# A two-layer MoE network with a gated recurrent mixer: the recurrent mixer's last projections, GpSimd's order and the start of the output projections are rearranged

## What is computed

```python
def short_conv_mixer(xn, w_in, conv_w, w_out):            # layer 0
    bgate, cgate, h = jnp.split(xn @ w_in, 3, axis=-1)
    u = depthwise_conv(cgate * h, conv_w, (1, 1))
    return (bgate * u) @ w_out

def rglru_direction(uh, w_r, b_r, w_i, b_i, lam, reverse):
    r = sigmoid(einsum(uh, w_r) + b_r)                    # blocks of 256 channels
    i = sigmoid(einsum(uh, w_i) + b_i)
    log_a = -RG_C * r * softplus(-lam)
    a = exp(log_a)
    gated = sqrt(-expm1(2 * log_a)) * (i * u)
    return associative_scan(_linear_combine, (a, gated), reverse=reverse)

def rglru_mixer(xn, ...):                                 # layer 1
    y_branch, u = jnp.split(xn @ w_in, 2, axis=-1)
    y_branch = gelu(y_branch)
    u = depthwise_conv(u, conv_w, (2, 1)) + conv_bias
    h = rglru_direction(uh, ..., False) + rglru_direction(uh, ..., True)
    return (y_branch * h) @ w_out

for i in range(DEPTH):
    h = h + mix
    h = h + hier_moe(rmsnorm(h, norm_ffn[i]), ...)        # 32 experts, three 2 MB matrices each
    h = h + sigmoid(rmsnorm(h, norm_ple[i]) @ w_ple_gate[i] + b) * (p[i] @ w_ple[i])
```

## Time and profile before

| | us |
|---|---|
| median of 3 runs | 2106.71 |
| lowest and highest | 2106.17, 2112.98 |
| the profiled execution, its own time | 2108.99 |
| its span | 2107.2 |
| TensorE busy | 1968.6 (93%) |
| layer 0's mixer ends, output projection begins | 190.9 |
| layer 1's mixer, first full projection block to last | 848 to 1018 |
| layer 1's output projection begins | 1021.2 |
| layer 1's experts begin | 1105.8 |

### The profile page before, as it was taken

One profiled execution on the slowest core, in us unless ns is written; L12 is line 12 of the kernel. 1 busy time (PEld: TensorE's weight loads), 2 busy tenths in 40 slices (PEclk: granted clock), 3 DMA queues, 4 the chain that ended last, 5 costly groups with the idle time before them and its releaser, 6 DMA issues.

```text
span 2107.2 us, 21306 instructions
## 1 busy us (share of the span) xinstructions
PE 1968.6 (93%) x8286; PEld 970.6 (46%) x8286; DVE 760.3 (36%) x2018; ACT 419.0 (20%) x871; POOL 100.8 (5%) x128
## 2 busy tenths in 40 slices
PE   7999999999999799988999999999979899998997
PEld 3444555444444235433464444444424564644554
DVE  3111353221111143454345421111115448656674
ACT  2000010111110124166111111111013432113342
POOL 0000000000000010013300000000010000000000
PEclk9999989999999999999999999999989999996999
DMA  6187179999999981210537999999995212210000
GB/s 276 40 166 280 60 301 402 429 427 429 428 428 428 421 340 40 74 46 0 248 141 326 405 428 429 427 428 428 428 398 232 85 71 80 80 40 1 17 15 11
DMA packets 46323, 512.79 MB, mean 243 GB/s; under 512 B 5248, under 2 KB 5248, under 8 KB 17152
## 3 DMA queue, kind: packets, MB, share of 16 engines
q1 hardware_dynamic: 37760, 481.38, 56.1%
q0 software_dynamic: 8448, 29.89, 3.6%
HBM read 484.90 MB, written 26.35 MB: 243 GB/s over the span
## 4 chain that ended last, share of the span: by engine, by line
PE 80%; DVE 7%; DMA 6%; issue 4%; ACT 2%; POOL 1%; SPq 0%; DVEq 0%; POOLq 0%
PE ps L925 20%; PE ps L964 9%; PE ps L468 8%; PE ps L898 7%; PE ps L562 5%; PE ps L1316 5%; PE ps L1750 5%; DMA ring<-in_wexp 4%; PE ps L1479 3%; PE ps L2068 3%; PE ps L1510 2%; PE ps L1949 2%; PE ps L989 1%; PE ps L2112 1%; PE ps L2086 1%
## 5 line engine op out<-in xcount | busy, mean ns | idle before, releaser
L925 PE MATMUL ps<-ring,arena 128*48 128x512 f32 x1568 | 404.5, 604 | 43.1 <-issue 28.6
L925 PEld LDWEIGHTS ps<-ring,arena 128*48 128x48 f32 x1568 | 121.7, 125 | 243.9 <-issue 242.4
L938 DVE TENSOR_TENSOR arena<-arena,ps 48x512 f32<-48x512 f32 x64 | 44.1, 690 | 465.9 <-ACT arena L932 465.8
L964 PE MATMUL ps<-ring,arena 128*48 128x512 f32 x800 | 181.7, 592 | 2.4 <-issue 2.4
L898 PEld LDWEIGHTS ps<-arena,h 128*128 128x128 f32 x1024 | 158.6, 190 | 44.6 <-issue 44.6
L898 PE MATMUL ps<-arena,h 128*128 128x192 f32 (+1 forms) x1024 | 174.3, 325 | 0.0
L468 PE MATMUL ps<-arena,ring 128*128 128x512 f32 x384 | 165.0, 592 | 1.0 <-DVE arena L305 1.0
L925 PE MATMUL ps<-arena 128*48 128x512 f32 x480 | 159.4, 612 | 1.0 <-issue 1.0
L1750 PE MATMUL ps<-ring,arena 128*128 128x512 f32 (+3 forms) x384 | 135.2, 507 | 0.0
L932 ACT ACTIVATE arena<-ps 48x512 f32<-48x512 f32 x64 | 37.9, 592 | 479.6 <-PE ps L925 467.6
L562 PE MATMUL ps<-ring,arena 128*128 128x512 f32 x256 | 115.7, 608 | 7.0 <-DVE arena L500 3.9
(11 more groups left out here) (278 smaller groups left out, 2112.3 us busy)
## 6 DMA issues: line engine op xcount, KB each, us to landing
ring<-in_wexp SPq DMA_DIRECT2D x148, 2048.0 KB, 19.6
arena<-in_wexp SPq DMA_DIRECT2D x44, 2048.0 KB, 22.6
ring<-in_wall SPq DMA_DIRECT2D x28, 2048.0 KB, 8.6
y_d<-arena POOLq DMA_DIRECT2D x60, 192.0 KB, 7.1
yo_d<-arena SPq DMA_DIRECT2D x2, 4032.0 KB, 42.0
xs_d<-h POOLq DMA_DIRECT2D x8, 512.0 KB, 3.9
ring<-in_wall SPq DMA_DIRECT2D x2, 1536.0 KB, 6.8
h<-in_x SPq DMA_DIRECT2D x4, 512.0 KB, 9.5
```

What stands on the lines that cost most here:

```text
L925: mm = pe.matmul(outs[m], xeT[:, e_ // 4 % 2, k, e_ % 4 * CAP:(e_ % 4 + 1) * CAP], ws[m][:, k, :], start=(k == 0), stop=(k == KT - 1))
L938: dve.tensor_tensor(hh[0:CAP, e_ % 2, :], sl[0:CAP, e_ % 2, :], banks[1][64:64 + CAP, :], ALU.mult).then_inc(S["hh"], 1)
L964: mm = pe.matmul(outs[c], hT_of(e_ % 2)[:, k, :], w[:, k, c * 512:(c + 1) * 512], start=(k == 0), stop=(k == 3))
```

## The change

Three edits, in source order.

1. `pe_out` (both layers) no longer waits for all eight channel blocks ahead of the first product. Instead each of the eight matmuls of `product(0, 0)` waits for the block that it reads, with a floor: layer 0 waits for count 7 before the first seven and for 8 before the last; layer 1 waits for 5 before the first five, then for 6, 7 and 8. The floor is what frees PSUM bank 0.
2. `pe_mixer_b`: the first channel block of the y quarter (block 8 for d = 0, block 12 for d = 1) is computed in the middle of the gates, after c = 3. The other three blocks stay behind the gates.
3. `pool_mixer_b`: the first four products L1614 move in front of the last four sums, and the last four products alternate with them: sum 4, product 4, sum 5, product 5, and so on.

No instruction but waits is added or taken away.

```diff
--- before.py
+++ after.py
@@ -559,10 +559,11 @@
                 if i >= 1:
                     pe.wait_ge(S["op_add"], 8 * k + 2 * i + c - 1)
                 for kk in range(KT):
+                    if i == 0 and c == 0:
+                        pe.wait_ge(*((S["b_y"], max(kk + 1, 5)) if k else (S["a_gT"], max(kk + 1, 7))))
                     mm = pe.matmul(banks[c][:], gT[:, kk, i * P:(i + 1) * P], w[:, kk, :], start=(kk == 0), stop=(kk == KT - 1))
                 mm.then_inc(S["op_mm"], 1)
 
-            pe.wait_ge(S["b_y"] if k else S["a_gT"], 8)
             product(0, 0)
             product(0, 1)
             turn_half(pe, n, 0, 0)
@@ -1466,10 +1467,10 @@
             for key in (("b", 0), ("b", 1), ("gates", 0), ("b", 2), ("gates", 1), ("b", 3)):
                 sp_load(sp, key)
 
-        def pe_project(pe, q, at=0):
+        def pe_project(pe, q, at=0, to=4):
             w = w8(("b", q))
             pe_unit(pe, ("b", q))
-            for c4 in range(at, 4):
+            for c4 in range(at, to):
                 p_ = 4 * q + c4
                 if 4 <= p_ < 12:
                     pe.wait_ge(S["bu"], p_ - 3)
@@ -1509,7 +1510,9 @@
                         for k in range(2):
                             mm = pe.matmul(banks[4 + g % 4][:], w[:, a, blk, k, m * P:(m + 1) * P], uc[:, 2 * blk + k, :], start=(k == 0), stop=(k == 1))
                         mm.then_inc(S["b_gm"], 1)
-                pe_project(pe, 2 + d)
+                    if c == 3:
+                        pe_project(pe, 2 + d, 0, 1)
+                pe_project(pe, 2 + d, 1)
 
         def act_mixer_b(act):
             for c in range(8):
@@ -1596,22 +1599,34 @@
                         o.then_inc(S["b_sc"], 1)
 
         def pool_mixer_b(pool):
-            for d in range(2):
-                for hf in range(2):
-                    for cc in range(4):
-                        c = 4 * hf + cc
-                        k = 8 * d + c
-                        pool.wait_ge(S["b_gs"], 2 * k + 2)
-                        pool.tensor_tensor(bI[hf][:, cc, :], bI[hf][:, cc, :], uc[:, c, :], ALU.mult).then_inc(S["b_iu"], 1)
-                    if d == 1:
-                        for cc in range(4):
-                            c = 4 * hf + cc
-                            pool.wait_ge(S["b_sc"], 8 + c + 1)
-                            pool.tensor_tensor(hs[:, c, :], hs[:, c, :], bT[:, cc, :], ALU.add).then_inc(S["b_hs"], 1)
-            for c in range(8):
+            def gated(d, hf):
+                for cc in range(4):
+                    c = 4 * hf + cc
+                    k = 8 * d + c
+                    pool.wait_ge(S["b_gs"], 2 * k + 2)
+                    pool.tensor_tensor(bI[hf][:, cc, :], bI[hf][:, cc, :], uc[:, c, :], ALU.mult).then_inc(S["b_iu"], 1)
+
+            def both(c):
+
+                pool.wait_ge(S["b_sc"], 8 + c + 1)
+                pool.tensor_tensor(hs[:, c, :], hs[:, c, :], bT[:, c % 4, :], ALU.add).then_inc(S["b_hs"], 1)
+
+            def product(c):
                 pool.wait_ge(S["by"], c + 1)
                 pool.wait_ge(S["b_hs"], c + 1)
                 pool.tensor_tensor(yT[:, c, :], yT[:, c, :], hs[:, c, :], ALU.mult).then_inc(S["b_y"], 1)
+
+            gated(0, 0)
+            gated(0, 1)
+            gated(1, 0)
+            for c in range(4):
+                both(c)
+            gated(1, 1)
+            for c in range(4):
+                product(c)
+            for c in range(4, 8):
+                both(c)
+                product(c)
 
 
         QK = ar(4096, 17, 512)
```

## The result

| | before | after |
|---|---|---|
| median, us | 2107.9 (4 runs) | 2091.94 (4 runs) |
| lowest and highest | 2106.17, 2112.98 | 2084.6, 2094.43 |
| ratio of the times, 95% interval | | 0.9917 [0.9899, 0.9936] |
| the profiled execution, its own time | 2108.99 | 2084.6 |

A second session gave the changed kernel 2095.19 us (6 runs) against 2109.15, ratio 0.9935 [0.9914, 0.9955]. By the medians it is 16.0 and 14.0 us faster; 15.1 was forecast. The two intervals together reach from 9.5 to 21.3 us. The profiled execution is the fastest of its four and must not be read as the result: its span is 24.4 us shorter.

The account below looks back on a forecast made before the run. TensorE, busy 1968.6 of 2107.2 us, was taken as the bound, leaving only gaps and low clock to win. 5.7 (layer 0) + 9.4 (layer 1) = 15.1 us off the 2106.71 median gave 2091.6 us; range 2084 to 2098 (8 in 10).

Parts of the forecast that it names:

- What decides: Layer 1's output projection: product(0, 1) waits for the load of ("out", 1, 1), used at 1016.9 instead of 1029.16, 12.3 us earlier.
- The gates: Layer 1's gates: blocks 8 and 12 fill both 6.20 us gaps, saving 9.0 and 9.4 us.
- The close fit: Direction 0's gates: block 8 and four groups cover TensorE until ScalarE's first sigmoid, 0.65 us to spare.
- The last product: End of layer 1's mixer: GpSimd's last product brings b_y to 8 at 1008.8, 12.3 us earlier than 1021.1.
- The turns: Last half of layer 1's mixer: each GpSimd op ahead of a waiting VectorE op delays it 0.95 us, 10.0 in all.
- cheaper-pairs rival: Last half's L1582 and L1584 don't take turns with GpSimd; last product at 1003.6, time 2086.5 us; chance 0.15.
- Issue to use: Layer 1's second output-weight load: 8.04 us from the DMA's issue to its use by product(0, 1).
- Low clock behind the new gap: Layer 1's product(0, 1): after 7.1 us idle it runs partly at 1.2 GHz, costing 2.9 us, range 1.5 to 4.
- layer 1 term: Layer 1's output projection: 12.3 us from the earlier load less 2.9 of low clock, net 9.4 us.
- Layer 0: Layer 0's output projection: the 3.9 us gap and 1.8 us of slow clock go, 5.7 us.
- absorbing rival: Expert stages: a DMA start that doesn't move swallows one or both gains, 2101.0 to 2106.7 us; chance 0.09.
- The clock stays low: Rival, layer 1's output products: 1.2 GHz persists for the seven remaining products, 48.1 us more, 2136.8 us; chance 0.05.

Follow-up runs that it names:

- e2_layer1: Only the finer waits of edit 1, in layer 1 alone, against the kernel before: 2108.42 us, ratio 0.999.
- e5_slot: Changed kernel with the second half of layer 1's output weights in ring slot 3 instead of slot 2: 2085.48 us, ratio 0.9886.
- e3_blocks: Only edit 2, the projection block between the halves of the gates, against the kernel before: 2096.58 us, ratio 0.9936.
- e7_oldpool: Changed kernel with GpSimd's old order, so edits 1 and 2 without 3: 2092.58 us, ratio 0.9912.
- e6_slot_oldpool: Changed kernel with the output weights' second half in ring slot 3 and GpSimd's old order: 2091.82 us, ratio 0.9915.
- e4_gpsimd: Only edit 3, GpSimd's new order, against the kernel before: 2106.62 us, ratio 0.9981.
- e8_dve: Against e5_slot, the eight products with the y branch run on VectorE, four behind each half's scans: 2083.57 us, ratio 0.987.
- e1_layer0: Only the finer waits of edit 1, in layer 0 alone, against the kernel before: 2103.93 us, ratio 0.9967.
- e9_dve_noslot: As e8_dve, but the output weights' second half stays in the slot that counts as used until the last product: 2086.41 us, ratio 0.9881.

## Why the prediction was right, point by point

- **What decides.** The step on which the forecast stood, that the load of ("out", 1, 1) ends the wait, holds: the bracket is in the profile (6.51 us forecast as about 7), e2_layer1 shows the early start worth nothing alone, and e5_slot wins 6.7 us of stage by giving this load another slot.
- **The gates.** 9.0 and 9.4 us, right to some tenths: from the first gate matmul to the first output product are 990.33 - 880.47 = 109.9 us, and 999.6 - 889.5 = 110.1 was forecast. The close fit held, no bracket opened.
- **The last product.** 1008.8 forecast in the times of the kernel before; measured 1000.0, which is 1009.1 with the 9.06 us by which the first gate matmul moved. The turns were forecast to cost 10.0 us ahead of the last scan's end, and the lengthened ops there add up to 10.2. The price of 0.95 us was right for the pairs too, which no row had shown: five long ops of 1.64 to 1.76 in the pairs. With it the cheaper-pairs rival falls. The rule of the Trainium skill (SBUF — State Buffer, Who interferes with whom), that an op with two SBUF inputs excludes a GpSimd op that reads SBUF, agrees with the trace: L1587's 1.65 for 0.69 us is the row that was missing. The lengthening, 0.95 to 1.08 us, is less than GpSimd's whole 1.25.
- **Issue to use.** 8.04 taken, 7.67 measured.
- **Low clock behind the new gap: mis-sized.** The term was 2.9 us, the mean of two gaps of 6.20; it measured 8.71 - 7.03 = 1.7, and 1.7 again in the second profile. A similar gap cost 2.6 (e2_layer1, 4.18 us), a longer one 2.8 (e3_blocks). The length of a gap does not fix this price: 7.29 us in front of the same matmuls cost 2.9 us in e7_oldpool and 1.8 in e6_slot_oldpool. The forecast's own range for the term, 1.5 to 4, held it. The first matmul of product(0, 1) moved by 12.8 us instead of 12.3: the last product came 0.3 us later than forecast, the load was used 0.4 sooner behind its issue, and the matmul now starts with its weight load, where it stood 0.4 behind it before. Together the layer 1 term is 11.1 instead of 9.4.
- **Layer 0: mis-sized the other way.** The two products won the forecast 5.7 us, but the stage to the experts 3.8 to 6.7, because in five of nine profiles 1.6 or 1.7 us were lost again at a new stretch of low clock further on. The forecast had put 2 us either way on the router's low clock; it was mostly one way, and the new stretches lie ahead of the router's end.
- **Behind it.** The experts run against a full DMA and still passed the gain on: with edit 1 in layer 0 the stage is 611.3 us in the mean against 612.1, and layer 1's expert stage is 561.7 in the mean of the nine profiles with edit 2 against 561.0 in the four without. The absorbing rival falls.
- **The clock stays low: fell.** It rose about 3.3 us behind product(0, 1)'s start, near 1011.0.
- **The sum.** Stage terms measured: 3.8 to 6.7 and 11.1, together 14.9 to 17.8; the two sessions gave 16.0 and 14.0 us between the medians. The hit is partly luck: layer 1's term was 1.7 us too small and layer 0's in most profiles 1.7 to 1.9 too large. The first profile alone, 24.4 us, would have been misleading, since about 7.7 of it lie in the expert stages, which vary by as much between profiles.
- **GpSimd's order.** By the prediction its 8.6 us are eaten by 10.0 us of turns, some of which were there before. That holds for the last product, which comes only 1.3 us sooner by it. That even this is lost, because the gap changes its place and with it the place of the low clock, was not foreseen: e7_oldpool's stage came out 0.3 us shorter than the changed kernel's.

## What to carry to other kernels

When a wait is split into finer ones, ask of the next instruction behind the first finer one what it waits for: here the second product's weights lay in a slot that the same count frees, and the early start was worth nothing until that load was moved. Before work is moved into an engine's idle time, look at which other engine runs there: four products moved to VectorE took 5.69 us instead of 2.5, because GpSimd ran at that moment. And compare stages by distances inside one profile, for two profiles of one kernel differed by 7.5 us in stages that no edit touched. When two stretches of clock are compared across kernels, put the windows at the same instructions and not at the same times.

## What the runs showed of the hardware

- GpSimd's elementwise ops and VectorE's lengthen each other as if they took turns, also where VectorE's is the combined op with two tensors (0.69 alone, 1.65 beside GpSimd), and not only for products and scans (0.68 to 1.76, 1.22 to 2.17). It costs VectorE 0.95 to 1.08 us for each GpSimd op of 1.25, and GpSimd's op grows to 1.63 to 2.00.
- The low clock came behind single gaps as short as 2.03 (e4_gpsimd) and 2.15 us (e8_dve), and behind two gaps of 1.76 and 1.50 us with two records between them (e5_slot). Single gaps of 1.19 and 1.83 us were followed by 16 records in 7.13 instead of 7.03 us, at the full clock, and gaps of 0.43 and 0.49 us did nothing.
- Gaps of 2.03, 2.15, 3.14, 3.88, 4.18, 6.20, 6.5 and 10.86 us were followed by 1.8, 1.8, 1.5, 1.8, 2.6, 2.2 to 3.1, 1.7 and 2.8 us of loss, and 7.29 us by 1.8 and 2.9: no order by length (the one of 6.5 us stands behind two shorter ones). What differs is how long after TensorE's restart the clock rose: about 3.3 us in the changed kernel (loss 1.7), 3.5 in e6_slot_oldpool (1.8), 5.8 in e7_oldpool (2.9), so about half of that time was lost.
- In layer 0's output stage a short stretch of low clock appeared on the same instructions in some kernels and not in others, far from any gap over 0.8 us: in 16 small matmuls in e1_layer0 and e5_slot (3.55 for 1.92 us), in a product some 20 us ahead of them in e7_oldpool, e8_dve and e9_dve_noslot (8.73 for 7.03), in none of the other eight profiles.
